# NSA first, RWKV second: the RWKV projection between the causal NSA units, z by way of DRAM, gate projections inside the turns of the RWKV heads

## The reference, cut to what matters

```python
h = rms_norm(x, norm_mix_pre)
z = h @ w_in                                   # 3360 RWKV + 2608 NSA + 2048 gate columns
z_rwkv, z_nsa, z_gate = jnp.split(z, [RWKV_COLS, RWKV_COLS + NSA_COLS], axis=-1)
o_a = rwkv7_time_mix(z_rwkv, ...)              # z + (prev - z) * mu, then 16 heads of 64, a scan over the tokens
o_b = nsa_attention(z_nsa, ...)                # 16 heads: compressed, selected and window attention
g_a, g_b = jnp.split(jax.nn.sigmoid(z_gate), 2, axis=-1)
m = g_a * (o_a @ w_branch_rwkv) + g_b * (o_b @ w_branch_nsa)
x = x + rms_norm(m @ w_out, norm_mix_post)
x = x + ffn(rms_norm(x, norm_ffn_pre))         # untouched
```

## Time and profile before

| | |
|---|---|
| time, median of 3 runs | 3635.32 us (3634.15 to 3637.9) |
| the profiled execution | 3634.61 us, span 3632.8 us |
| mean granted TensorE clock | 0.864 |
| PE busy | 2978.4 us, 82% |
| PEld busy | 1926.4 us, 53% |
| DVE busy | 2407.1 us, 66% |
| ACT busy | 1237.8 us, 34% |
| POOL busy | 618.6 us, 17% |

### The profile page before, as it was taken

How to read it: one execution, slowest core, us unless ns; L and a number is a source line. 1 busy time by engine, 2 the same in 40 slices (tenths; PEclk the granted TensorE clock), 3 DMA queues, 4 the chain that set the end, 5 groups by cost and what they waited for, 6 DMA issues and landing times. The chain is left out here.

```text
span 3632.8 us, 59338 instructions
## 1 busy us (share of the span) xinstructions
PE 2978.4 (82%) x22748; PEld 1926.4 (53%) x22859; DVE 2407.1 (66%) x4206; ACT 1237.8 (34%) x2024; POOL 618.6 (17%) x413
## 2 busy tenths in 40 slices
PE   7696985559999999997786777777685999669987
PEld 4353453446666666675335656666444455334466
DVE  3794299977787788787427778775453555448742
ACT  2232132563333333332333334332201555323320
POOL 0460043113343333332000000000000222100000
PEclk9658997779999999998997788776795999889998
DMA  3002232368989989984400000000411110323240
GB/s 108 7 1 83 86 114 91 149 250 307 330 309 327 331 309 327 328 316 151 159 36 1 2 2 2 2 1 1 133 33 44 53 48 25 116 77 115 69 128 30
DMA packets 236125, 454.03 MB, mean 125 GB/s; under 512 B 15104, under 2 KB 145536, under 8 KB 234272
## 3 DMA queue, kind: packets, MB, share of 16 engines
q1 hardware_dynamic: 199072, 317.21, 24.8%
q0 software_dynamic: 36864, 134.23, 10.4%
HBM read 415.74 MB, written 35.65 MB: 124 GB/s over the span
## 5 line engine op out<-in xcount | busy, mean ns | idle before, releaser
L1314 PE MATMUL banks<-gated_hi,v_lo 128*128 128x384 bf16 (+2 forms) x1536 | 335.0, 273 | 0.0
L1314 PE MATMUL banks<-gated_lo,v_hi 128*128 128x384 bf16 (+2 forms) x1536 | 335.0, 273 | 0.0
L1314 PE MATMUL banks<-gated_hi,v_hi 128*128 128x384 bf16 (+2 forms) x1536 | 335.0, 273 | 0.0
L1301 PE MATMUL banks<-act_hi,u_hi 128*128 128x384 bf16 x768 | 252.1, 328 | 22.9 <-DVE u_lo L1236 22.9
L1147 POOL DMA_INDIRECT gathered_v<-in_v,first_tile_rows x128 | 177.0, 1383 | 499.6 <-DVE x_tokens L1250 470.6
L1301 PE MATMUL banks<-act_lo,u_hi 128*128 128x384 bf16 x768 | 252.0, 328 | 0.0
L1301 PE MATMUL banks<-act_hi,u_lo 128*128 128x384 bf16 x768 | 251.9, 328 | 0.0
L1142 POOL DMA_INDIRECT gathered_u<-in_u_rows,first_tile_rows x128 | 156.7, 1224 | 205.8 <-POOLq L986 146.7
L1314 PEld LDWEIGHTS banks<-gated_hi,v_hi 128*128 128x128 bf16 x1536 | 150.3, 98 | 55.4
L1250 DVE SCALAR_TENSOR_TENSOR x_tokens<-gathered_v,gathered_weights,x_tokens 128x1024 f32<-128x1024 f32 x128 | 164.2, 1282 | 10.3 <-DVE gathered_weights L1241 3.1
L1314 PEld LDWEIGHTS banks<-gated_hi,v_lo 128*128 128x128 bf16 x1536 | 139.5, 98 | 38.9
(11 more groups left out here) (618 smaller groups left out, 8319.5 us busy)
## 6 DMA issues: line engine op xcount, KB each, us to landing
v_raw<-in_v SPq DMA_DIRECT2D x128, 512.0 KB, 11.9
u_raw<-in_u SPq DMA_DIRECT2D x96, 512.0 KB, 11.6
gate_tables<-gate_piece SPq DMA_DIRECT2D x12, 2048.0 KB, 6.3
gate_group<-gate_tables SPq DMA_DIRECT2D x32, 768.0 KB, 16.0
ffn_up_raw<-in_ffn_up SPq DMA_DIRECT2D x20, 1024.0 KB, 7.5
early_u_raw<-in_u SPq DMA_DIRECT2D x32, 512.0 KB, 3.7
rwkv_in_raw<-in_w_in SPq DMA_DIRECT2D x5, 2048.0 KB, 8.3
ffn_down_raw<-in_ffn_down SPq DMA_DIRECT2D x3, 2816.0 KB, 14.0
```

What stands on the lines that cost most here:

```text
L1301: m = pe.matmul(ps[:, SCORE_BANK + (slot + j) % 2, 0:DT], u[:, j, d, :], x[:, d, P:], start=(d == 0 and n == 0), stop=(d == KD - 1 and n = ...
L1314: m = pe.matmul(ps[:, bank, to:to + width], v[:, j, cols], w[:, j, tok:tok + width], start=start and n == 0 and to == 0, stop=stop and n = ...
```

## The change

The two mixers change places, and dense work is placed beside other work than before.

- `nsa_projection`, `nsa_compress` and `nsa_compressed_attention` come first, right behind the one normalization that is left.
- The causal stage, now `nsa_causal_and_rwkv_in`, fills its units with the 27 tiles of the RWKV projection (27 x 24 = 648 products, in place of 576) by `DENSE_PER_UNIT`. ScalarE copies a finished bank times mu, VectorE mixes it, and SP stores that tile of z to DRAM. `rwkv_projection` is gone.
- `nsa_out_to_parts` has no sigmoids or gate products any more; it stores both parts of the NSA output to DRAM. All semaphores are cleared once more behind it.
- `rwkv_squash` loads z's last three tiles from DRAM. In `rwkv_heads` SP loads z and the low-rank weights pair by pair, two pairs in SBUF. The turns are written out one by one instead of a hardware loop. The 16 tiles of gate logits (384 products) are made inside: twelve products ahead of a turn, and three before and three after each stage's second product, in bank 5; ScalarE casts and empties, GpSimd subtracts, and the logits go to DRAM. For that, the two products of a stage share banks 2 and 3, and the grams rotate over three banks.
- `merge_branches` makes both branch products (384 products in place of 192), in four chunks whose four pieces alternate between the two matrices, with the sigmoid of the logits as ScalarE's step; the loads of the logits stand behind the first chunk's.
- The second normalization is gone. x is loaded back at the end of the heads.

```diff
+DENSE_PER_UNIT = (7, 6, 5, 3)
...
-def rwkv_projection(k, z, tables):
...
+def rwkv_squash(k, z, tables):
+    landed, squashed = k.sem("z_low_rank_landed"), k.sem("z_low_rank_squashed")
     with k.nc.Block() as block:
+        @block.sync
+        def _(sp):
+            for n in range(RZ - 3 * KD):
+                rows = min(P, RW_COLS - (3 * KD + n) * P)
+                sp.dma_start(z[0:rows, n, :], k.dram["z"][3 * KD + n, 0:rows]).then_inc(landed, 16)
+            tables.load(k, sp)
         @block.scalar
         def _(act):
-            act.activation(z[0:64, 24, :], z[0:64, 24, :], ACT.Tanh)
-            act.activation(z[:, 25, :], z[:, 25, :], ACT.Sigmoid)
-            act.activation(z[0:32, 26, :], z[0:32, 26, :], ACT.Sigmoid)
+            act.wait_ge(landed, 16 * (RZ - 3 * KD))
+            act.activation(z[0:64, 0, :], z[0:64, 0, :], ACT.Tanh)
+            act.activation(z[:, 1, :], z[:, 1, :], ACT.Sigmoid)
+            act.activation(z[0:32, 2, :], z[0:32, 2, :], ACT.Sigmoid).then_inc(squashed, 1)
+            act.wait_ge(squashed, 1)
...
+    for i in range(1, KD - 1):
+        turn(i, i % 2, invert=True, chained=True, prepare=True)
...
+                def load_pair(j):
+                    if j >= 2:
+                        steps.wait("prepare", "vector", j, "columns", before=2)
+                        steps.wait("prepare", "scalar", j, "v", before=2)
+                        steps.wait("prepare", "tensor", j, "gate", before=2)
+                    for n in range(3):
+                        sp.dma_start(z2[:, j % 2, n, :], k.dram["z"][j + n * KD]).then_inc(z_landed[j % 2], 16)
+                    cols = slice(j * P, (j + 1) * P)
+                    w = wj2[:, j % 2]
+                    for dst, src in ((w[0:64, 0, :], k.dram["rwkv_w2_2"][:, cols]), (w[64:P, 0, :], k.dram["rwkv_a2_2"][:, cols]),
+                                     (w[:, 1, :], k.dram["rwkv_g2_2"][0:P, cols]), (w[0:32, 2, :], k.dram["rwkv_g2_2"][P:, cols])):
+                        sp.dma_start(dst, src).then_inc(wj_landed[j % 2], 16)
+                def load_gate(p):
+                    if p >= 3:
+                        sp.wait_ge(w_low, p - 2)
+                    c, half = divmod(p, 2)
+                    at0 = first_gate + half * D + c * P
+                    sp.dma_start(raw[:, p % 3], w_in[:, :, at0:at0 + P]).then_inc(w_landed[p % 3], 16)
+                def store_gate(p):
+                    sp.wait_ge(evicted, p + 1)
+                    sp.dma_start(k.dram["gate_logits"][p], logits[:, p % 2, :]).then_inc(stored[p % 2], 16)
+                load_pair(0)
                 sp.dma_start(k.dram["kept_x"].rearrange("(t p) d -> p t d", p=P), k.x[:]).then_inc(spilled, 16)
+                for p in range(3):
+                    load_gate(p)
+                load_pair(1)
                 sp.wait_ge(spilled, 16)
+                for i in range(KD):
+                    if i >= 1 and i + 1 < KD:
+                        load_pair(i + 1)
+                    if i >= 1:
+                        store_gate(2 * i - 1)
+                    for p in (2 * i + 3, 2 * i + 4):
+                        if p < 2 * KD:
+                            load_gate(p)
+                    store_gate(2 * i)
+                steps.wait("finish", "vector", KD - 2, "out")
+                for n in range(2):
+                    sp.dma_start(nsa_out[n], k.dram["nsa_parts"][:, n]).then_inc(nsa_back, 16)
+                store_gate(2 * KD - 1)
                 names = RW_NAMES["chain"]["tensor"]
                 sp.wait_ge(sems["chain", "tensor"], len(names) * KD)
                 sp.dma_start(k.x[:], k.dram["kept_x"].rearrange("(t p) d -> p t d", p=P)).then_inc(back, 16)
                 sp.wait_ge(back, 16)
+                sp.wait_ge(nsa_back, 32)
+                for n in range(2):
+                    sp.wait_ge(stored[n], 16 * KD)
             @block.gpsimd
             def _(pool):
...
                 pool.memset(G2[0], 0.0).then_inc(cleared, 1)
                 pool.wait_ge(spilled, 16)
                 pool.memset(G2[1], 0.0).then_inc(cleared, 1)
...
+                for p in range(2 * KD):
+                    pool.wait_ge(w_high, p + 1)
+                    pool.tensor_tensor(wl[:, p % 2], raw[:, p % 3], wh[:, p % 2], ALU.subtract).then_inc(w_low, 1)
...
+                def gate_high(p):
+                    act.wait_ge(w_landed[p % 3], 16 * (p // 3 + 1))
+                    if p >= 2:
+                        act.wait_ge(multiplied, p - 1)
+                    act.copy(wh[:, p % 2], raw[:, p % 3]).then_inc(w_high, 1)
+                def gate_out(p):
+                    act.wait_ge(multiplied, p + 1)
+                    if p >= 2:
+                        act.wait_ge(stored[p % 2], 16 * (p // 2))
+                    act.copy(logits[:, p % 2, :], ps[:, 5, :]).then_inc(evicted, 1)
...
+                        if invert and s == 3:
+                            gate_out(2 * i)
...
+                        if invert and s == 1 and i >= 1:
+                            gate_high(2 * i + 1)
+                        if invert and s == 4 and i + 1 < KD:
+                            gate_high(2 * i + 2)
+                    if invert:
+                        gate_out(2 * i + 1)
...
-                    busy = [("vector", "columns"), ("scalar", "tok0"), ("scalar", "tok1"), ("scalar", "tok2"),
+                    steps.wait("prepare", "vector", j, "columns")
+                    busy = [("scalar", "tok0"), ("scalar", "tok1"), ("scalar", "tok2"),
                             ("vector", "gram00"), ("vector", "gram01"), ("vector", "gram10"), ("vector", "gram11"),
-                            ("vector", "gram20"), ("vector", "gram21")]
+                            ("vector", "gram20"), ("vector", "gram21"), ("vector", "low_part00")]
...
+                    for _ in range(count):
+                        p, m = divmod(dense_done[0], NM)
+                        d, n = divmod(m, 3)
+                        if m == 0:
+                            pe.wait_ge(w_low, p + 1)
+                            if p >= 1:
+                                pe.wait_ge(evicted, p)
+                        w, x = ((wh, k.xh), (wh, k.xl), (wl, k.xh))[n]
+                        ins = pe.matmul(ps[:, 5, :], w[:, p % 2, d, :], x[:, d, :], start=m == 0, stop=m == NM - 1)
+                        if m == NM - 1:
+                            ins.then_inc(multiplied, 1)
+                        dense_done[0] += 1
...
+                        dense(DENSE_FIRST)
...
                         if invert:
+                            dense(DENSE_PASSES)
                             xlx(i, slot, s)
...
+                        if invert:
+                            dense(DENSE_PASSES)
...
-RW_GRAM_BANKS = [5, 2, 3, 4, 5, 2]
-RW_LOW_BANKS = [3, 4, 5, 2]
-def nsa_projection(k, q, ckv, ks, kw, v, gl, raw):
+RW_GRAM_BANKS = [2, 3, 4, 2, 3, 4]
+RW_LOW_BANKS = [2, 3, 4, 2]
+DENSE_FIRST = 12
+DENSE_PASSES = 3
...
+    NP, NM = RZ, 3 * KD
+    mu = COLUMN_AT["rwkv_mu_2"]
+    ka = COLUMN_AT["rwkv_k_a_2"]
+    asked = [0 if u < 2 else DENSE_PER_UNIT[units[u][1]] for u in range(NU)]
+    ends = [min(sum(asked[:u + 1]), NP * NM) for u in range(NU)]
     assert ends[-1] == NP * NM
+    counts = [e - s for s, e in zip([0] + ends, ends)]
     last_unit = [min(u for u in range(NU) if ends[u] >= NM * (p + 1)) for p in range(NP)]
...
+                for p in range(3):
+                    load(p)
+                for p in range(NP):
+                    if p + 3 < NP:
+                        load(p + 3)
+                    sp.wait_ge(mixed, p + 1)
+                    sp.dma_start(k.dram["z"][p, 0:width(p)], zout[0:width(p), p % 3, :]).then_inc(stored[p % 3], 16)
+                for n in range(3):
+                    sp.wait_ge(stored[n], 16 * (NP // 3))
...
+                def move(p):
                     act.wait_ge(multiplied, p + 1)
-                    act.copy(kept[p], ps[:, 6 + p % 2, :]).then_inc(evicted, 1)
+                    if p >= 2:
+                        act.wait_ge(mixed, p - 1)
+                    rows = slice(0, width(p))
+                    act.activation(shifted_z[rows, p % 2, 1:], ps[rows, 6 + p % 2, :], ACT.Copy,
...
+                def mix(p):
+                    dve.wait_ge(moved, p + 1)
+                    if p >= 3:
+                        dve.wait_ge(stored[p % 3], 16 * (p // 3))
+                    rows = slice(0, width(p))
+                    dve.scalar_tensor_tensor(zout[rows, p % 3, :], ps[rows, 6 + p % 2, :], k.one_less[rows, p:p + 1],
+                                             shifted_z[rows, p % 2, 0:S], ALU.mult, ALU.add).then_inc(mixed, 1)
...
+            for n, part in enumerate((hi, lo)):
+                sp.wait_ge((high, low)[n], KD)
+                sp.dma_start(k.dram["nsa_parts"][:, n], part[:]).then_inc(stored, 16)
+            sp.wait_ge(stored, 32)
...
+        def source(c):
```

(25 more changed lines are left out.)

303 lines of the change are left out of this document (141 added, 162 removed).

## The result

The changed kernel takes 3548.2 us (median of 4 runs, 3539.8 to 3551.6) against 3636.4 for the kernel before beside it: a ratio of 0.9755, interval 0.9736 to 0.9774. That is 88 us faster. It lies inside the range, 23 us above the forecast of 3525. The profiled execution took 3550.5 us.

A forecast was written before the change was run, and what follows sets the result against it. TensorE, busy 2978.4 of 3632.8 us, sets most stages; in the heads it and VectorE hand work to each other. Terms -155.9 - 16.0 + 16 + 0 + 3.5 - 3 + 45 = -110.4 give 3525 us, range 3494 to 3560.

The forecast's parts named there:

- Book of products, and what is removed: 1416 products before and after, TensorE spared none; the projection stage (-155.9 us) and second normalization (-16.0) go.
- Causal stage: 72 more products beside mixes and copies, in the causal NSA stage: +16 us, bounds +15 and +27.
- NSA parts, squash, branch product: Stages around the heads: parts 0 us (-1 to +3), squash +3.5 (+2 to +6), branch product +45 (+42 to +52).
- Heads: RWKV heads stage, sum of four terms: 2 - 5 - 11 + 11 = -3 us, bounds -25 and +35.
- start: Start of the heads: z and pair 0's small weights are loaded inside the block, +2 us.
- loop: In the heads, the loop over pairs of turns becomes straight code; three long turns shorten: -5 us.
- gate products and clock: In the heads' turns, 48 products each mostly hidden, faster TensorE clock, three gram banks: -1.4 us a turn, -11 in eight.
- splits: In the heads, GpSimd splits 16 gate tiles and delays VectorE's masked copies: +11 us, range 0 to +34.
- (a): Clock wins: TensorE stays at 2.4 GHz through the turns, few splits hit VectorE; heads -21, whole 3507 us; chance 0.18.
- (b): Gate work lands on the heads' path: products cost 28 us, splits 12; heads +37, whole 3565 us; chance 0.17.
- (c): Causal stage stops being TensorE's, 72 products cost 27 us, branch product's start at upper bound; whole 3543; chance 0.10.
- (d): Gates find no room in the heads and run at the slow level: 164 us, whole 3689; chance 0.02.

The follow-up runs named there:

- the pair without splits: Changed kernel without GpSimd's 16 subtractions of gate tiles, once with 32 and once with 384 gate products: heads 674.1 and 671.0 us.
- the moved casts: Changed kernel with ScalarE's gate-tile casts moved, so GpSimd's subtractions fall where VectorE is idle or in its reciprocal; no work left out: 3515.1 us, ratio 0.9659.

## Why the prediction was right in sign and range, and 23 us too fast

**Book of products, and what is removed.** Right. The stages that went were worth the 171.9 us that stood in their rows.

**Causal stage.** +16 forecast, +20.0 found, inside the bounds of 15 and 27. TensorE still sets it, clock 0.97. VectorE's new mixes show as 22.6 us more busy time, beside it.

**NSA parts, squash, branch product.** 0, +3.5 and +45 forecast; -0.2, +2.5 and +42.1 found. The branch product's start cost less than the +3.6 put down for it: 42.1 less the 41.4 of its products leaves 0.7.

**Heads.** The step that failed. Its terms:

- start, +2 forecast: +2.6 from the stage's begin to the first turn. Six of the eleven profiles of this code have 6 instead, when the clearing meets VectorE; that this one doesn't is luck.
- loop, -5 forecast: -10 in the heads of one profile. The sign was right; the size is open, as the runs don't resolve it.
- gate products and clock, -11 forecast (bounds -22 and 0). The direction of the clock is right: it rose, to 0.87 to 0.93 in the turns without splits, and the products cost no time. The size is wrong: the pair without splits tells -3.1 (674.1 to 671.0; -6.8 with the accident of the start taken off), and by itself the bank rotation costs 6.7, which that term had inside. Together that is about zero to +4, some 11 to 15 over the forecast. The loop's -10 hid part of it.
- splits, +11 forecast: +32.0 by the run without them, +34.7 by the moved casts. This is the term that was mis-sized most. The forecast took one microsecond a split where VectorE is critical, two times in three. Every split hit a copy of VectorE's (15 of 16 a masked one), at 1.6 us on average, because both casts stand right behind a stage's last copies on ScalarE, and so each split starts with VectorE's growth step. The walk through the turn had the two at the same place and then gave them odds. It had no term at all for what the wait does to TensorE's clock.

The term's bounds, 0 to 34 us, were used up: 32.0, 34.7, or some 36 with the accident of the start taken off. By the Trainium skill, "SBUF — State Buffer", section "Who interferes with whom", the text had a sum of 3548, and the measured time is 3548.2. That close a hit is partly chance: the stretches were 26 us and not 34, the clock's part of the loss was in no rule, and the products gained less and the loop more than forecast. But the rule was to be taken at full price.

The heads' stated upper bound, +35, doesn't follow from the terms as given (2 - 5 + 0 + 34 = 31). The 1 to 2 us for a further clearing of semaphores rests on no row; the stage that has it came out 0.2 us shorter as a whole.

**Its signs.** Of those for right, masked copies near 2 us and a clock over 0.8 came; the causal stage (305.5 at 0.97, for 301 at 0.98), the heads (703.0, for 660 to 700) and the turns (78.4 to 85.2, for 76 to 79) lay above, the branch product (95.1, for 98) below. Three of those for wrong came as well, each in part: one turn of 85.2 us; TensorE waiting 4.9 us for a low half, once, in turn 0; and causal heads of over 19 us, four of fifteen, at 19.0 to 19.4.

**Rivals.** (a), the clock wins, is what the moved casts show: heads 14 us under those of before, 3515 in all, where it said 21 and 3507. It failed here in the main by the splits. (b), heads at +37 for the +20.7 found, has its halves the wrong way round: the products it charged with 28 us pay instead, and the splits it charged with 12 cost 32. (c) put +27 on the causal stage and +52 on the branch product, 7 and 10 too much; its 3543 lies nearest to the measured time of all the rivals, by luck. (d) is out: without the products the kernel is slower.

The sum of single edits doesn't close to the microsecond. Before, less 10.4 for the loop, plus 6.7 for the banks and 2.6 for the start, is 681.2, and the kernel with neither splits nor products has 674.1. The 7 us between are not assigned; single turns scatter by some 5 us.

## What to carry to other kernels

When work is given to GpSimd beside VectorE, look up which VectorE instructions will run in those microseconds, and find one of the same kind beside a GpSimd instruction in a trace. Counting inputs is not enough: masked copies, a plain copy and a one-tensor arithmetic operation were held up by a split, a reciprocal was not. Here one order of two casts on ScalarE was worth 33 us of 3548, with no instruction more or less. Dense products put into TensorE's idle stretches can be worth more than they cost, so the time without them is a test and not a lower bound. A collision found in a walk through the schedule is to be counted at its full price, if producer and victim are released by the same engine one instruction apart.

## What the runs showed of the hardware that was not expected

- 352 products of 512 columns taken out of the heads made them 32 us longer (703.0 to 735.1); the granted clock of a turn fell from 0.88 to 0.72.
- A split costs more than the stretched instruction: 1.6 us of stretch and 2.0 to 2.2 us of time with products beside it (32.0 and 34.7 for 16), 4.1 without (49.4 us in six turns, 12 splits).
- A 3.35 us reciprocal with one input took 3.35 us with a 2.13 us split inside it; masked copies took 1.9 to 2.6 in place of 0.69. Cut in four, a split takes 3.5 us in place of 2.1, and two copies take 1.06 and 1.18.
- One input doesn't protect: beside a split a plain copy took 2.35 us in place of 0.42, and a one-tensor TENSOR_SCALAR 2.35 in place of 0.42. A GpSimd MEMSET of 2.66 us, which reads nothing, made a one-tensor TENSOR_SCALAR 2.89 us in place of 0.55 and left a TENSOR_TENSOR with two tensors at 0.69. That collision comes in six of eleven profiles, and their stage starts are 3.7 us longer.
